# A matmul step of the RWKV branch and a chain step moved within one layer's written order

## The chip, the cores and the metric

The kernel runs on one core of a Trainium2 chip, out of eight. The metric is the device time of one execution in microseconds (us). The engines are TensorE (PE: matmul; PEld: its weight loads, which overlap), VectorE (DVE), ScalarE (ACT), GpSimd (POOL) and SyncE (SP), which issues the DMAs. They run at the same time, each through its own list of instructions in the order written, and wait for each other by semaphores. Matmul results go to PSUM, eight banks of 128 x 512 fp32.

## The reference

Two decoder layers over 512 positions of width 1024. Each layer takes an RMS norm, projects to 4160 columns, feeds four groups of heads, gates each with SiLU, and projects back with a residual:

```
h = rmsnorm(x, norm_w);  proj = h @ w_in
y_rwkv = rwkv7_time_mix(...) * silu(gate)     # 4 heads of 64
y_conv = short_conv_mix(...) * silu(gate)
y_moba = moba_attention(...) * silu(gate)     # causal, T5 bias
y_ret  = retention_chunkwise(...) * silu(gate)
x = x + concat(y_rwkv, y_conv, y_moba, y_ret) @ w_out
```

A final RMS norm follows. The RWKV group is a recurrence over time with a 64 x 64 state per head:

```
s_kk = state @ kk_t
state = state * w_t - s_kk (kk_t * a_t)^T + v_t k_t^T
y_t = state @ r_t
```

## The kernel before, in words

The activations are kept transposed in SBUF, as a rounded high part and a rest (act_hi, act_lo), and so are the weights (w_hi, w_lo). A projection of 128 columns is therefore 3 x 8 matmuls of 128 x 512 into one PSUM bank, in lines 773, 775 and 776. SyncE streams the weights; ScalarE (line 1286) and GpSimd (line 707) split them. The projections alternate between banks 0 and 1. Banks 2 to 7 serve the small work of the four groups.

The order of the work is written out by hand in layer_steps(). It returns one list of steps per layer, and each engine walks through the same list, doing its own part of every step that it has a function for. The second half of the list is made of slots: each of the last sixteen projections is cut into four quarters of six matmuls (step quarter), two quarters to a slot; mid[i] holds the steps between the two quarters of slot i, and after[i] those behind the second. Steps put in these places run on TensorE between products.

The RWKV recurrence is computed in 8 chunks of 64 positions. The steps that matter here:

- chunk_q (line 1077) computes two tiles q0 and q1, in banks 6 and 5. VectorE adds them to the queries in the step queries (line 1887); its four additions are line 1894. c = 0 reads q0, c = 1 reads q1, and each signals the bank as read behind its second addition.
- chunk_y1 (line 1080, by_chunk, lines 1104 and 1105) adds the two state-free terms of the output into y0 (bank 5) and y1 (bank 6), 64 small fp32 matmuls. It needs no result of the chain. Before the first matmul it calls begin for both banks.
- chain(c), c = 1 to 6, (line 1109 for TensorE, 1897 for VectorE) carries the state from chunk to chunk: four 64 x 64 matmuls into bank 7 (line 1121), then two multiply-adds on VectorE (line 1901), and the next chain step waits for them.
- chunk_y (line 1124) adds the state's part to y0 and y1. It waits for chain(6).

The attention runs in six units u: attend_scores(u) (TensorE line 1009, VectorE lines 1817 and 1822, ScalarE's exponential, line 1455), attend_norm(u) (VectorE, lines 1829 and 1832), attend_turn(u) (TensorE transposes, line 1020, evicted by ScalarE in line 1461), attend_values(u) (line 1036) and, after the last unit of a pair of heads, attend_out (VectorE, line 1840). Units 0 and 3 hold query blocks 0 and 1, units 1 and 4 block 2, units 2 and 5 block 3.

Which job uses a bank, and how often the bank must have been filled and read before, is counted by bank_jobs() in the order of the steps. The count makes a wait: begin(job) lets TensorE wait until every earlier job of the bank has been read:

```
def begin(job, layer):
    b, nf, nr, _ = locate(job, layer)
    if nr > 0:
        pe.wait_ge(bank_read[b], nr)
    return bank[b]
```

In slots 16 to 18 the list before the change reads: quarter(cc0, 0), attend_norm(2), queries, quarter(cc0, 1), quarter(cc0, 2), chain(5), attend_turn(2), quarter(cc0, 3), conv_c(0), attend_values(2), attend_out(0), attend_scores(3), chunk_y1, chain(6), quarter(cc1, 0), attend_norm(3), quarter(cc1, 1), quarter(cc1, 2), attend_turn(3), quarter(cc1, 3). Here cc0 and cc1 are two projections of the convolution group.

Of the kernel before, what the change touches and what calls it, by code (L numbers as in the profile page):

```python
# [108 lines left out]
UNITS = 2 * len(PARTS)  # L109
# [32 lines left out]
def layer_steps():  # L142

    s = [("k_pair",)]
    s += [("shift", "k0"), ("shift", "k1"), ("kk_input",), ("shift", "wa"), ("shift", "r0"), ("kk_square",),
          ("kk_norm",), ("kk_unit", 0), ("lora_tanh",), ("shift", "r1"), ("kk_unit", 1), ("lora",), ("shift", "v0"), ("decay_scan",), ("shift", "v1"),
          ("decay_exp",), ("factors", 0), ("gate", "rwkv", 0), ("factors", 1), ("gate", "rwkv", 1), ("factors", 2)]

    s += [("copy", "rq0"), ("copy", "rq1"), ("bonus",), ("rotate", "rq0"),
          ("copy", "rk0"), ("rotate", "rq1"), ("scores", 0), ("scores", 1), ("copy", "rk1"), ("rotate", "rk0"), ("to_rows", "v"), ("scores", 2),  # L150
          ("scores", 3), ("wide", 0, 0), ("wide", 0, 1), ("rotate", "rk1"), ("wide", 0, 2), ("wide", 0, 3),
          ("to_rows", "kap"), ("to_rows", "bet"), ("block_rows", 0), ("wide", 1, 0), ("wide", 1, 1), ("wide_out", 0), ("wide_out", 1),
          ("to_rows", "alp"), ("block_rows", 1), ("wide", 1, 2), ("wide", 1, 3), ("wide_out", 2), ("wide_out", 3), ("to_rows", "rk"),
          ("block_rows", 2)]

    last = [("gate", "ret", 0), ("gate", "ret", 1)] + [("copy", j) for j in ("mq0", "mk0", "mq1", "mk1")] + [("gate", "moba", 0), ("gate", "moba", 1)]
    last += [("conv_c", 0), ("conv_c", 1), ("conv_h", 0), ("conv_h", 1), ("conv_b", 0), ("conv_b", 1), ("gate", "conv", 0), ("gate", "conv", 1)]
    slots = 2 * len(last)  # L160
    mid, after = [[] for _ in range(slots)], [[] for _ in range(slots)]
    after[0] += [("retain_state",), ("retain_scores", 0), ("retain_scores", 1)]
    after[1] += [("centre_v",), ("inverse_eye",)]
    after[2] += [("retain_values",), ("retain_out", 0), ("retain_out", 1)]
    after[5] += [("ret_low",)]
    for i, step in [(INV0, ("inverse_x",)), (INV0, ("chunk_b",)),
                    (INV0 + 1, ("inverse_y",)), (INV0 + 1, ("inverse_yt",)),
                    (INV0 + 3, ("corner_x",)), (INV0 + 4, ("corner_t",)), (9, ("ret_stat",)), (10, ("chunk_uw",)),
                    (11, ("chunk_gh",)), (21, ("ln_square",)), (22, ("ln_var",))]:
        mid[i].append(step)  # L170
    for c in range(1, NCH - 1):


        if c % 2:
            mid[12 + c].insert(0, ("chain", c))
    after[9] += [("ret_root",), ("ret_recip", 0)]
    for u in range(UNITS + 1):


        if u > 0:  # L180
            mid[11 + 2 * u].append(("attend_turn", u - 1))
            after[11 + 2 * u].append(("attend_values", u - 1))
            if u % 3 == 0:
                after[11 + 2 * u].append(("attend_out", u // 3 - 1))
        if u in (1, 2):
            after[11 + 2 * u].append(("chain", 2 * u))
        if u < UNITS:
            (after[11 + 2 * u] if u else mid[10]).append(("attend_scores", u))
        if u == 3:
            after[11 + 2 * u] += [("chunk_y1",), ("chain", 2 * u)]  # L190
        if u < UNITS:
            (mid[12 + 2 * u] if u else after[11]).append(("attend_norm", u))
    mid[15].insert(1, ("chunk_q",))
    mid[16].append(("queries",))
    after[19].append(("chunk_y",))
    for i, step in [(10, ("ret_recip", 1)), (11, ("ret_recip", 2)), (12, ("ret_recip", 3)), (13, ("ret_finish", 0)), (14, ("ret_finish", 1)),
                    (21, ("conv_taps", 0)), (24, ("conv_taps", 1)), (22, ("ln_recip", 0)), (23, ("ln_recip", 1)), (25, ("ln_recip", 2)), (26, ("ln_recip", 3)),
                    (26, ("ln_scale", 0)), (27, ("ln_scale", 1)), (28, ("rwkv_finish", 0))]:
        after[i].append(step)
    for i in range(slots):  # L200
        step, job = last[i // 2], project_name(last[i // 2])
        s += [("quarter", job, 2 * (i % 2))] + mid[i] + [("quarter", job, 2 * (i % 2) + 1)]
        if i < slots - 1:
            s += [step] * (i % 2) + after[i]

    s += [("split_y", k) for k in Y_ORDER[:4]] + [("rwkv_finish", 1), ("split_y", 0), last[-1], ("conv_out", 0), ("split_y", 1), ("conv_out", 1)]
    s += [("split_y", k) for k in Y_ORDER[6:]] + [("out", q) for q in range(5)] + [("out_end",)]
    return s
# [5 lines left out]
def project_name(step):  # L214

    kind = step[0]
    if kind == "gate":
        return f"{step[1]}_g{step[2]}"
    if kind in ("conv_c", "conv_h", "conv_b"):
        return {"conv_c": "cc", "conv_h": "ch", "conv_b": "cb"}[kind] + str(step[1])  # L220
    return step[1]


Y_ORDER = [6, 7, 4, 5, 0, 1, 2, 3]
ROW_ORDER = [3, 2, 0, 1]
STEPS = layer_steps()


# [1871 lines left out]
```

## Time and profile before

| | us |
|---|---|
| median of 3 runs | 582.18 |
| lowest and highest | 581.69, 582.97 |
| the profiled execution, whole | 581.69 |
| its span, first to last instruction | 579.9 |
| TensorE busy | 571.4 |
| VectorE busy | 370.6 |
| ScalarE busy | 275.1 |
| GpSimd busy | 249.7 |

The profile is of one execution. Times in it count from the first instruction, so 1.8 us of the execution's time lie outside its span. The first layer takes the first half, the second the rest; the place of the change is near 195 us in the first layer and near 476 us in the second. Ends of matmuls are modelled and overlap the next start.

### The profile page before, as it was taken

To read this page: it belongs to the slowest core of one execution; us is meant where nothing else is said; L and a number is where in the kernel's file an instruction comes from. 1 tells how busy PE (TensorE), PEld (TensorE's weight loads), DVE (VectorE), ACT (ScalarE), POOL (GpSimd) and SP (SyncE) were. 2 spreads that over 40 slices of the span, in tenths; PEclk is the share of its full clock that TensorE was granted. 3 is DMA by queue.
4 is the path that set the end of the run, shared out by engine and by line. 5 is a ranking of instruction groups with operands and counts; after the bars stand their busy time and mean duration, and the time that the engine had idled before them with its cause. 6 is when DMAs were issued, how large, how long until landed. Compare 5 with 4: busy or idle time off the path is not lost. (4 is left out here: it accounts for less than half of the span.)

```text
span 579.9 us, 12191 instructions
## 1 busy us (share of the span) xinstructions
PE 571.4 (99%) x4988; PEld 467.2 (81%) x4988; DVE 370.6 (64%) x624; ACT 275.1 (47%) x551; POOL 249.7 (43%) x197
## 2 busy tenths in 40 slices
PE   9999999999999999999999999999999999999995
PEld 7978888888777777888898788888878778788884
DVE  4999975582276747774544897946434874778163
ACT  6485331345273565534657643324536334745253
POOL 5846451045923313436335555402395313145340
PEclk9999999999999999999999999999999999999999
DMA  9556725056422122353534433422744121224513
GB/s 283 160 153 184 227 74 119 0 129 148 110 76 73 43 68 58 113 170 135 163 121 133 110 85 98 108 48 85 153 112 111 37 74 40 72 73 146 181 41 141
DMA packets 103372, 64.61 MB, mean 111 GB/s; under 512 B 29152, under 2 KB 94228, under 8 KB 103189
## 3 DMA queue, kind: packets, MB, share of 16 engines
q1 hardware_dynamic: 103316, 63.83, 39.5%
q8 instruction: 40, 0.66, 0.5%
q14 instruction: 16, 0.12, 0.1%
HBM read 55.68 MB, written 8.14 MB: 110 GB/s over the span
## 5 line engine op out<-in xcount | busy, mean ns | idle before, releaser
L707 POOL TENSOR_TENSOR w_lo<-w_raw,w_hi 128x512 fp32r<-128x512 f32 x156 | 217.2, 1412 | 291.4 <-ACT w_hi L1286 290.0
L773 PE MATMUL bank<-act_hi,w_hi 128*128 128x512 f32 x432 | 173.1, 401 | 0.0
L776 PE MATMUL bank<-act_lo,w_hi 128*128 128x512 f32 x432 | 168.5, 390 | 0.3 <-issue 0.3
L775 PE MATMUL bank<-act_hi,w_lo 128*128 128x512 f32 x416 | 162.3, 390 | 0.0
L1286 ACT ACTIVATE w_hi<-w_raw 128x512 fp32r<-128x512 f32 x140 | 80.2, 621 | 73.7 <-PE bank L858 28.2
L773 PEld LDWEIGHTS bank<-act_hi,w_hi 128*128 128x128 f32 x432 | 81.1, 188 | 24.3 <-issue 7.8
L776 PEld LDWEIGHTS bank<-act_lo,w_hi 128*128 128x128 f32 x432 | 81.1, 188 | 18.0 <-issue 0.7
L775 PEld LDWEIGHTS bank<-act_hi,w_lo 128*128 128x128 f32 x416 | 78.2, 188 | 14.8
L1212 PE MATMUL bank<-w_hi,act_hi 128*128 128x512 f32 x128 | 50.0, 391 | 0.0
L1214 PE MATMUL bank<-w_hi,act_lo 128*128 128x512 f32 x128 | 49.8, 389 | 0.0
L1213 PE MATMUL bank<-w_lo,act_hi 128*128 128x512 f32 x128 | 49.8, 389 | 0.0
L1985 DVE TENSOR_TENSOR x_or_y<-x_or_y,bank 128x512 f32<-128x512 f32 x16 | 11.0, 688 | 37.5 <-PE bank L1214 37.5
L1394 ACT ACTIVATE pages<-bank 128x512 f32<-128x512 f32 x16 | 9.5, 596 | 42.1 <-PE bank L776 42.1
L1214 PEld LDWEIGHTS bank<-w_hi,act_lo 128*128 128x128 f32 x128 | 24.0, 188 | 5.0
L1212 PEld LDWEIGHTS bank<-w_hi,act_hi 128*128 128x128 f32 x128 | 24.0, 188 | 5.0
L1213 PEld LDWEIGHTS bank<-w_lo,act_hi 128*128 128x128 f32 x128 | 24.0, 188 | 4.9
L1455 ACT ACTIVATE pages<-pages,small 128x128 f32<-128x128 f32 (+3 forms) x32 | 17.9, 559 | 18.6 <-DVE small L1822 18.6
L1752 DVE SCALAR_TENSOR_TENSOR x_or_y<-x_or_y,bank 128x512 f32<-128x512 f32 x16 | 10.9, 683 | 23.6 <-ACT x_or_y L1360 23.4
L856 PE MATMUL bank<-w_hi,act_hi 128*128 128x512 f32 x64 | 25.5, 398 | 0.0
L858 PE MATMUL bank<-w_hi,act_lo 128*128 128x512 f32 x64 | 25.0, 390 | 0.0
L857 PE MATMUL bank<-w_lo,act_hi 128*128 128x512 f32 x64 | 24.9, 390 | 0.0
L1817 DVE SCALAR_TENSOR_TENSOR pages<-bank,bias 128x128 f32<-128x128 f32 (+3 forms) x32 | 14.7, 481 | 16.0 <-PE bank L1009 15.7
(217 smaller groups left out, 949.7 us busy)
## 6 DMA issues: line engine op xcount, KB each, us to landing
w_raw<-in_w_in_dram SPq DMA_DIRECT2D x62, 512.0 KB, 4.0
w_raw<-in_w_out_dram SPq DMA_DIRECT2D x16, 512.0 KB, 3.8
pages<-in_x_dram SPq DMA_DIRECT2D x4, 512.0 KB, 6.0
x_or_y<-in_x_dram SPq DMA_DIRECT2D x4, 512.0 KB, 4.0
x_scratch<-x_or_y SPq DMA_DIRECT2D x4, 512.0 KB, 2.9
x_or_y<-x_scratch SPq DMA_DIRECT2D x4, 512.0 KB, 3.7
out_dram<-pages SPq DMA_DIRECT2D x8, 256.0 KB, 2.2
bias_scratch<-pages SPq DMA_DIRECT2D x1, 1280.0 KB, 7.9
```

The costliest lines, as they stand in the source:

```text
L707: ins = pool.tensor_tensor(low, raw, w_hi[:, i % HI, k, 0:n].bitcast(F32), ALU.subtract)
L773: mm(b[:, :], hi, act_hi[:, k, :], start=n == 0, stop=False)
L775: mm(b[:, :], lo, act_hi[:, k, :], start=False, stop=False)
L776: ins = mm(b[:, :], hi, act_lo[:, k, :], start=False, stop=n == KT - 1)
L856: mm(o, act_hi[:, n, tc], w_hi[:, :, n, :], start=n == 0, stop=False)
L857: mm(o, act_hi[:, n, tc], w_lo[:, :, n, :], start=False, stop=False)
L858: ins = mm(o, act_lo[:, n, tc], w_hi[:, :, n, :], start=False, stop=n == KT - 1)
L1212: mm(b[:, :], act_hi[:, k, tc], hi[:, wc], start=first, stop=False)
L1213: mm(b[:, :], act_hi[:, k, tc], lo[:, wc], start=False, stop=False)
L1214: ins = mm(b[:, :], act_lo[:, k, tc], hi[:, wc], start=False, stop=last)
L1286: go(w_hi[:, i % HI, k, 0:n], w_raw[:, i % RAW, k, 0:n], ACT.Copy).then_inc(s("w_high"), 1)
L1455: go(pb, pb, ACT.Exp, bias=row_max[:, n:n + 1], accum_out=row_sum[:, n:n + 1]).then_inc(s("prob"), 1)
```

## The change

chunk_y1 moves from behind attend_scores(3) in after[17] to mid[17], between chain(5) and attend_turn(2). chain(6) stays in after[17], but now stands ahead of attend_scores(3) in place of behind it and chunk_y1. The list of slot 17 then reads: quarter(cc0, 2), chain(5), chunk_y1, attend_turn(2), quarter(cc0, 3), conv_c(0), attend_values(2), attend_out(0), chain(6), attend_scores(3), quarter(cc1, 0). attend_norm keeps its place. The counts of the banks follow the list: y0 and y1 are still the jobs behind q1 and q0 in banks 5 and 6.

```diff
@@ -166,7 +166,7 @@
-                    (11, ("chunk_gh",)), (21, ("ln_square",)), (22, ("ln_var",))]:
+                    (11, ("chunk_gh",)), (17, ("chunk_y1",)), (21, ("ln_square",)), (22, ("ln_var",))]:
         mid[i].append(step)
@@ -182,13 +182,10 @@
-        if u in (1, 2):
+        if u in (1, 2, 3):
             after[11 + 2 * u].append(("chain", 2 * u))
         if u < UNITS:
             (after[11 + 2 * u] if u else mid[10]).append(("attend_scores", u))
-        if u == 3:
-            after[11 + 2 * u] += [("chunk_y1",), ("chain", 2 * u)]
-        if u < UNITS:
             (mid[12 + 2 * u] if u else after[11]).append(("attend_norm", u))
```

## Rows read from the trace of the kernel before

**Rows 1.** The page: busy us, share and count; granted TensorE clock in 40 slices.

```profile
PE 571.4 (99%) x4988; PEld 467.2 (81%) x4988; DVE 370.6 (64%) x624; ACT 275.1 (47%) x551; POOL 249.7 (43%) x197
...
PEclk9999999999999999999999999999999999999999
```

**Rows 2.** Waits of TensorE, whole span: who <- for whom: us, times, longest.

```profile
PE bank L741 <- POOL pages L681: 1.0, 1, 1.0
PE bank L1102 <- issue: 0.7, 1, 0.7
PE bank L776 <- issue: 0.3, 1, 0.3
```

**Rows 3.** Timeline of TensorE, first layer: start us, us, engine, line, tiles, count.

```profile
194.44 0.45 PE L1121 MATMUL bank<-pages 64*64 64x64 f32 x8
194.82 1.09 PE L1020 MATMUL bank<-constants,pages 128*128 128x128 f32 x8
...
197.24 1.10 PE L1036 MATMUL bank<-pages 128*64 128x128 f32 x16
198.26 0.88 PE L1009 MATMUL bank<-pages 64*64 64x128 f32 x16
198.96 0.33 PE L1104 MATMUL bank<-pages 64*64 64x64 f32 x6
...
200.82 0.22 PE L1121 MATMUL bank<-pages 64*64 64x64 f32 x1
...
200.94 0.34 PE L1121 MATMUL bank<-pages 64*64 64x64 f32 x5
201.21 0.50 PE L773 MATMUL bank<-act_hi,w_hi 128*128 128x512 f32 x1
...
205.44 0.82 PE L1020 MATMUL bank<-constants,pages 128*128 128x128 f32 x6
```

**Rows 4.** Timeline of VectorE there; one stretch: us, busy (x), clock, DMA, GB/s.

```profile
194.49 1.41 DVE L1894 TENSOR_TENSOR pages<-pages,bank 128x256 f32<-128x256 f32 x4
195.82 0.47 DVE L1901 SCALAR_TENSOR_TENSOR pages<-bank,chunk_decay,pages 128x64 f32<-128x64 f32 x2
...
198.38 0.69 DVE L1840 SCALAR_TENSOR_TENSOR x_or_y<-bank,x_or_y 128x512 f32<-128x512 f32 x1 [2.08 <-PE bank L1036]
199.19 0.62 DVE L1817 SCALAR_TENSOR_TENSOR pages<-bank,bias 128x128 f32<-128x128 f32 x2
...
201.55 0.47 DVE L1901 SCALAR_TENSOR_TENSOR pages<-bank,chunk_decay,pages 128x64 f32<-128x64 f32 x2
...
202.79 0.55 DVE L1832 TENSOR_SCALAR pages<-pages,small 128x128 f32<-128x128 f32 x2
...
190.28:195.90 5.62, 5.19 (x13) 1.00 0.37 96
```

**Rows 5.** Timeline, second layer: two places where TensorE waits for another engine.

```profile
496.67 0.87 ACT L1461 ACTIVATE pages<-bank 128x384 f32<-128x384 f32 x2
...
497.68 0.88 PE L1036 MATMUL bank<-pages 128*64 128x128 f32 x12
...
504.04 0.49 DVE L1832 TENSOR_SCALAR pages<-pages,small 128x512 f32<-128x512 f32 x1
...
504.58 0.42 PEld L1020 LDWEIGHTS bank<-constants,pages 128*128 128x128 f32 x4 [0.20 <-DVE pages L1832]
504.64 1.19 PE L1020 MATMUL bank<-constants,pages 128*128 128x128 f32 x8
```

**Rows 6.** Timelines of TensorE and of VectorE in the second layer.

```profile
475.47 0.45 PE L1121 MATMUL bank<-pages 64*64 64x64 f32 x8
...
475.52 1.41 DVE L1894 TENSOR_TENSOR pages<-pages,bank 128x256 f32<-128x256 f32 x4
```

**Rows 7.** TensorE by stretches at the end: us, busy (x), granted clock, DMA, GB/s.

```profile
575.00:576.00 1.00, 0.00 (x0) 1.00 0.99 379
...
578.00:579.90 1.90, 0.00 (x0) 0.50 0.53 201
```

## The prediction

> **What bounds the kernel now.** I read the page's busy shares first. TensorE is busy 99% of the span at a granted clock of 9 tenths or more in every slice, the next engine 64% [rows 1]. The list of waits by engine comes second. It names almost nothing for TensorE: 1.0 us at the start, and later one gap of 0.7 us and one of 0.3 us put down to its own issue [rows 2]. So nothing on another engine can shorten the kernel unless TensorE waits for it, and any new wait of TensorE is paid in full. The timeline of TensorE and of VectorE around the moved steps comes third, because records of TensorE overlap (128 of them, of 0.22 us each, start within 1.86 us in chunk_y1 [rows 3]): a short wait doesn't show as idle time, and I go by the starts.
>
> The change touches one place per layer. TensorE's order there is now [rows 3]: chain(5) from 194.44, attend_turn(2) from 194.82, six products, attend_values(2) from 197.24, attend_scores(3) from 198.26, chunk_y1 from 198.96, chain(6) from 200.82, products from 201.21, attend_turn(3) from 205.44. Afterwards it is chain(5), chunk_y1, attend_turn(2), products, attend_values(2), chain(6), attend_scores(3), products, attend_turn(3).
>
> **Part 1: the work moved.** No instruction is added or removed on any engine, and no DMA, no ScalarE, GpSimd or SyncE step moves. chunk_y1 is 64 fp32 calls, 128 records per layer; from its first start to chain(6)'s it takes 200.82 - 198.96 = 1.86 us [rows 3]. It takes this from its old place and pays it at the new one: 0 in the sum. The kinds of tile on TensorE change as often as before: chain(5) and chunk_y1 are both 64*64 tiles ahead of the 128*128 transposes, and chain(6) and attend_scores(3) are 64*64 ahead of products. The last chain record starts 0.15 us before what follows it in both places (194.44 + 0.45 - 0.22 = 194.67 against 194.82; 200.94 + 0.34 - 0.22 = 201.06 against 201.21). An exit behind the 128-column scores, with records of 0.28 us in place of 0.22, may cost 0.06 more; a joint of two 64*64 steps less may give as much back. I take 0, with bounds of -0.1 and +0.1 per layer.
>
> **Part 2: the wait that chunk_y1 takes with it.** chunk_y1 writes y0 into bank 5 and y1 into bank 6, and asks for both banks before its first matmul. The jobs before it in these banks are q1 (bank 5) and q0 (bank 6), and VectorE reads them in the step queries, the four additions of line 1894. At the old place they were long read: 195.90 against 198.96. At the new place TensorE arrives as soon as chain(5) is issued. chain(5)'s last record starts at 194.67, so chunk_y1 could start at 194.68. VectorE starts the four additions at 194.49 and ends them at 194.49 + 1.41 = 195.90 [rows 4]. The one that counts first in the code is the last one: bank 5 holds q1, the second pair read.
>
> VectorE can't be earlier. From 190.28 to 195.90 it works almost without a hole through attend_scores(2), attend_norm(2) and then queries, 5.19 us busy of 5.62 [rows 4], and everything upstream of chain(5) is untouched by the change, so these times stand.
>
> The price of the release: at 504.04 + 0.49 = 504.53 VectorE ends a normalisation that TensorE waits for; the weight load starts at 504.58 and the matmul at 504.64, so 0.05 us plus 0.06 [rows 5]. That gives a first chunk_y1 matmul at 195.90 + 0.11 = 196.01, and a stall of 196.01 - 194.68 = 1.33 us. The bounds: 1.2 us, if the weight load is the only cost and the tail of chain(5) is hidden behind it, and 1.5 us, if the restart of an empty array is as slow as the slowest restart in these rows (ScalarE ends at 496.67 + 0.87 = 497.54, TensorE starts at 497.68, 0.14) and a first record is longer besides. In the second layer chain(5) starts at 475.47, 0.05 us before the four additions at 475.52, exactly as in the first (194.44 and 194.49) [rows 6], so the stall is the same: 2 x 1.33 = 2.66 us.
>
> **What is queued behind the wait.** TensorE runs in its written order, so attend_turn(2) stands behind chunk_y1 and starts at about 196.01 + 1.86 + 0.15 = 198.02 in place of 194.82. ScalarE's eviction of the transposes, attend_values(2), the eviction of cc0 and its weight preparation all follow TensorE and move by the same 3.2 us, of which 1.86 comes back where chunk_y1 no longer stands. GpSimd and the weight loads only get more time.
>
> **Part 3: chain(6) ahead of attend_scores(3).** On TensorE it waits for chain(5)'s read on VectorE, which starts at 195.82 and ends by 196.3; it comes at about 201.5 then, so no wait. On VectorE the 0.4 us of chain(6) (201.55 to 201.94) move ahead of the scores. The gap from attend_scores(3) to attend_turn(3) on TensorE shrinks, and here a second wait could appear. I count from the start of attend_values(2), as 0. TensorE: scores start at 1.02 and chunk_y1, chain(6) and scores cost 3.97 before the products (201.21 - 197.24). Without chunk_y1's 1.86 that is 2.1, and attend_turn(3) comes 205.44 - 201.21 = 4.23 later, at 6.33; its second half, which needs the second head, some 0.3 later. VectorE: attend_out ends at 199.07 - 197.24 = 1.83 [rows 4], chain(6) at about 2.15, the scores then start at 2.16 in place of 199.19 - 197.24 = 1.95. The last normalisation ended at 202.79 + 0.55 = 203.34, so 6.10, of which some 0.2 us was for chain(6) standing in between; with 0.21 added and 0.2 taken off it ends at about 6.1. It is needed at about 6.6. Cover left: 0.5 us in place of 2.1. Cost 0; if the cover fails, no more than some 0.3 us per layer.
>
> **Downstream.** After attend_turn(3) all engines stand to each other as before. Nothing there stops for anything but its predecessors, which move with TensorE; the waits of rows 5 (496.67 to 497.68, and at 504.5) come from ScalarE and VectorE chains that start at TensorE's own scores. So the delay isn't given back.
>
> **The sum.** 0 + 2.66 + 0 = +2.7 us on the profiled execution: span 579.9 to 582.6, its time 581.69 to 584.35. The median of the runs is 0.49 above the profiled one, so 582.18 + 2.66 = 584.8 us.
>
> **The clock.** TensorE's granted clock is 1.00 around the place, and at the end of the kernel it is still 1.00 from 575 to 576, a whole microsecond in which TensorE has no matmul; in the last 1.9 us it is 0.50, that is 1.2 in place of 2.4 GHz [rows 7]. A pause of that length leaves the clock where it is, and the stall of 1.3 us is little longer, so by these rows it costs nothing beyond itself. The Trainium skill (TensorE: Matmul & The Clock Gate, "A second HAM failure mode: psum-queue depth-cycling") says that short repeated idle spells between matmul groups can make the clock swing between its two levels. This kernel would have only one more such spell per layer. By that rule the sum would be the one of the third rival; the traces so far don't bear it out.
>
> **Rivals.**
> 1. The wait isn't there, or VectorE is through in time: TensorE meets bank 5 free. It decides at 194.68, the moment that TensorE gets there; the trace has the read at 195.90, and VectorE has no work that could go. For it speaks only that I infer TensorE's arrival from records with modelled ends. Then only part 1 is left: -0.2 to +0.2, so 582.2 us, not slower. Chance 0.13, of which 0.04 faster by over 0.2% and 0.09 within it (0.2% is what a measurement of this kernel can tell from no change, here 1.2 us).
> 2. Part of the stall is repaid: TensorE's small waits behind it vanish because others gain time: the release of 0.14 us at 497.68, and at 504.64, where the transposes take 1.19 us in place of the 1.09 at 194.82 [rows 3, 5]. It would give 584.8 - 2 x 0.24 = 584.3 us. Against it: they start from TensorE itself. Chance 0.06.
> 3. More than the stall: attend_turn(3) comes before its normalised rows (+0.3 per layer, 585.4 us), or the clock falls to its lower level in the pause. The slow stretch at the end holds at least 1.9 us; the same after each stall would cost half of it, 0.95 per layer, and twice that much if it lasts twice as long: 584.8 + 1.9 = 586.7, up to 588.6 us. Chance 0.07 together.
>
> **Numbers.** The forecast holds 0.74 by itself, 583.9 to 585.7 (stall 1.2 to 1.5 us per layer, part 1 at +-0.1 per layer, and the runs' own spread of about 0.5). With rival 2 and the near half of rival 3 in it, the range of 583.4 to 586.0 holds a little over 0.8. Faster 0.04, same 0.09, slower 0.87.
>
> **What the profile of the changed kernel would show.** A wait of TensorE at line 1104 on VectorE's line 1894, about 1.1 us of idle time in each layer (less than the stall by the pipelined tail), and none before. VectorE's four additions at 194.5 as now. attend_turn(2) at about 198.0 in the first layer, cc1's first product at 202.5, 1.3 after 201.21, and everything from there 1.3 later; from the second place on 2.7 later. attend_turn(3) without a wait. I am wrong if line 1104 starts before 195.9, if line 1894 starts earlier, if a wait of TensorE behind the place is new or gone, or if the granted clock falls below 1.00 near 196.

## The result and the profile after

| | before | changed |
|---|---|---|
| median of the runs, us | 582.29 (4 runs) | 585.75 (4 runs) |
| lowest and highest | 581.69, 582.97 | 584.31, 586.02 |
| profiled execution, whole; span | 581.69; 579.9 | 585.21; 583.4 |

The ratio is 1.0054, with a 95% interval of 1.0037 to 1.0072: the change made the kernel 2.2 to 4.2 us slower. A second measurement of the same two kernels, on another occasion, gave 1.0049 (1.0037 to 1.0062). The forecast was 584.8 us, slower, in a range of 583.4 to 586.0.

In the changed kernel every line behind the edited lines has a number lower by 3: chunk_y1 is in lines 1101 and 1102, queries in 1891, the transposes in 1017, the products in 770, 772 and 773. The waits of TensorE over the whole span (who waited, for whom: us in total, times, longest), of the changed kernel; before's are [rows 2]:

```profile
PE bank L1101 <- DVE pages L1891: 2.1, 2, 1.1
PE bank L738 <- POOL pages L678: 1.0, 1, 1.0
PE bank L1099 <- issue: 0.7, 1, 0.7
PE bank L773 <- issue: 0.5, 1, 0.5
PE bank L1033 <- ACT pages L1458: 0.3, 2, 0.2
```

The first line is new and is the forecast one: chunk_y1 waits twice, once in each layer, for VectorE's additions that read q0 and q1. The timeline of TensorE at the first place, changed kernel, to be laid beside [rows 3]:

```profile
194.90 0.45 PE L1118 MATMUL bank<-pages 64*64 64x64 f32 x8
196.41 0.37 PE L1101 MATMUL bank<-pages 64*64 64x64 f32 x8 [1.06 <-DVE pages L1891]
...
198.57 1.17 PE L1017 MATMUL bank<-constants,pages 128*128 128x128 f32 x8
199.50 0.47 PE L770 MATMUL bank<-act_hi,w_hi 128*128 128x512 f32 x1
...
201.06 1.09 PE L1033 MATMUL bank<-pages 128*64 128x128 f32 x16
202.08 0.38 PE L1118 MATMUL bank<-pages 64*64 64x64 f32 x5
202.25 0.32 PE L1006 MATMUL bank<-pages 64*64 64x128 f32 x1
...
203.11 0.50 PE L770 MATMUL bank<-act_hi,w_hi 128*128 128x512 f32 x1
...
207.35 0.82 PE L1017 MATMUL bank<-constants,pages 128*128 128x128 f32 x6
```

and VectorE there, to be laid beside [rows 4]:

```profile
194.95 1.41 DVE L1891 TENSOR_TENSOR pages<-pages,bank 128x256 f32<-128x256 f32 x4
...
202.20 0.69 DVE L1837 SCALAR_TENSOR_TENSOR x_or_y<-bank,x_or_y 128x512 f32<-128x512 f32 x1 [5.45 <-PE bank L1033]
202.81 0.47 DVE L1898 SCALAR_TENSOR_TENSOR pages<-bank,chunk_decay,pages 128x64 f32<-128x64 f32 x2
203.25 0.62 DVE L1814 SCALAR_TENSOR_TENSOR pages<-bank,bias 128x128 f32<-128x128 f32 x2
...
206.62 0.55 DVE L1829 TENSOR_SCALAR pages<-pages,small 128x128 f32<-128x128 f32 x2
```

The four additions start 0.05 us behind chain(5), as before, and end at 196.36; chunk_y1 starts at 196.41. From chain(5) to cc1's first product it is 203.11 - 194.90 = 8.21 us in place of 201.21 - 194.44 = 6.77, so the place costs 1.44. The second place, by the same rows:

```profile
477.63 0.45 PE L1118 MATMUL bank<-pages 64*64 64x64 f32 x8
...
479.14 0.37 PE L1101 MATMUL bank<-pages 64*64 64x64 f32 x8 [1.06 <-DVE pages L1891]
...
481.31 1.09 PE L1017 MATMUL bank<-constants,pages 128*128 128x128 f32 x8
```

**A table that needs one idea.** TensorE issues the same matmuls in the same order outside the two places. So I subtract, record by record, the start in one trace from the start of the same record in the trace of before. The difference is flat wherever nothing differs and steps up where something is lost. The steps at the two places, and the difference outside of them, are:

| trace | ahead of place 1 | place 1 | between | place 2 | at the last matmul |
|---|---|---|---|---|---|
| before, second trace | +0.10 | 0.00 | +0.17 | 0.00 | +0.28 |
| changed | +0.45 | 1.46 | +0.25 | 1.35 | +3.52 |
| changed, second trace | -0.30 | 1.47 | +0.47 | 1.38 | +3.07 |
| chunk_y1 alone | +0.37 | 1.45 | +0.20 | 1.38 | +3.41 |
| chain(6) alone | +0.09 | 0.10 | +0.20 | 0.09 | +0.49 |
| queries first | -0.11 | 0.17 | +0.46 | 0.08 | +0.59 |
| chunk_y1 behind the transposes | +0.86 | 1.71 | +0.18 | 0.56 | +3.31 |
| the same, second trace | +0.56 | 1.43 | +0.04 | 0.54 | +2.58 |
| chunk_y1 earlier | +0.57 | 5.98 | +0.33 | 3.37 | +10.26 |
| the same, second trace | +0.69 | 4.63 | +0.30 | 4.78 | +10.38 |
| chunk_y1 late | +1.22 | 0.25 | +0.17 | 0.25 | +1.90 |

Place 1 is measured from 189.6 to 208.1 us of before's time, place 2 from 455.5 to 488.0; a row adds up to its last column within 0.05, which arises behind place 2. The two places of the change come to 2.81 and 2.85 us and repeat to 0.03. What lies ahead of place 1 doesn't repeat, not even between two traces of one kernel.

### The profile page after: what moved, and what is told of

The parts are those of the page before. It is cut to its first block and busy times, and to the rows that moved or that the text cites. A ratio compares the mean times of both kernels' runs of the same rounds, so it can differ in the third digit from the quotient of the medians.

```text
span 583.4 us, 12191 instructions
## 1 busy us (share of the span) xinstructions
PE 572.7 (98%) x4988; PEld 468.0 (80%) x4988; DVE 368.5 (63%) x624; ACT 275.4 (47%) x551; POOL 250.2 (43%) x197
## 5 line engine op out<-in xcount | busy, mean ns | idle before, releaser
L1357 ACT ACTIVATE x_or_y<-bank 128x512 f32<-128x512 f32 x16 | 9.6, 598 | 31.0 <-PE bank L773 31.0
```

## Experiments

Each ratio is to the kernel before, from runs on the same chip, with its 95% interval. "At the places" means the columns of the table above.

**1. chunk_y1 alone.** chain(6) goes back behind attend_scores(3).

```diff
-        if u in (1, 2, 3):
+        if u in (1, 2):
             after[11 + 2 * u].append(("chain", 2 * u))
         if u < UNITS:
             (after[11 + 2 * u] if u else mid[10]).append(("attend_scores", u))
+        if u == 3:
+            after[11 + 2 * u].append(("chain", 2 * u))
+        if u < UNITS:
```

> One half of the change: chunk_y1 moves to its new place, chain(6) stays behind attend_scores(3). Theory (the wait of chunk_y1 for the read of bank 5 is the whole price): a wait at chunk_y1's first matmul of about 1.1 us of idle time in each layer, its first start 1.51 us behind chain(5)'s, cc1's first product 1.35 to 1.45 us late per place, and the time 2.8 us above before (585.1), within 0.3 of the changed kernel. Rival A (the order of chain(6) and attend_scores(3) holds the part that the forecast of 2.66 lacks against the measured 3.46): the wait is the same but the time is only 2.0 to 2.3 above before.

Measured: 585.52 us, ratio 1.0057 (1.0044 to 1.0070); 1.45 and 1.38 us at the places, the same wait of 1.06. That is the whole change again. Rival A falls.

**2. chain(6) alone.** chunk_y1 stands behind attend_scores(3), chain(6) ahead of it.

```diff
-                    (11, ("chunk_gh",)), (17, ("chunk_y1",)), (21, ("ln_square",)), (22, ("ln_var",))]:
+                    (11, ("chunk_gh",)), (21, ("ln_square",)), (22, ("ln_var",))]:
...
+        if u == 3:
+            after[11 + 2 * u].append(("chunk_y1",))
+        if u < UNITS:
```

> The other half: chain(6) ahead of attend_scores(3), chunk_y1 behind it, where nothing waits for banks 5 and 6. Theory: no wait of TensorE at chunk_y1, products of cc1 at the same distance from attend_values(2) as before (3.97 us, within 0.1), time within 0.3 us of before (582.3). Rival A: 0.5 to 0.8 us above before. Rival B (the price belongs to the new neighbours of chunk_y1, not to the wait): no change either, so this run is for A.

Measured: 582.75 us, ratio 1.0006 (0.9997 to 1.0014), 0.10 and 0.09 us at the places, no wait at chunk_y1. The timed runs can't tell this from nothing (0.4 us by the medians, a little over the expected 0.3); the traces can, and it is 0.1 us per place.

**3. queries first.** The changed kernel, with VectorE's read of the banks moved up.

```diff
-    mid[16].append(("queries",))
+    mid[16].insert(0, ("queries",))
```

> The changed kernel, with the step queries ahead of attend_norm(2), so that VectorE reads q0 and q1 while it would otherwise come to the normalisation: its four additions should start near 193.5 and end near 194.9, just about when chain(5) is issued, and the normalisation ends 1.4 us later, near 196.0, before the transposes need it at 196.9. Theory (the wait is the price): the wait at chunk_y1 falls from 1.06 us to 0.3 or less per layer, and the time to within 0.6 us of before (582.3 to 582.9). Rival B (TensorE pays for chunk_y1 between chain(5) and the transposes, by tile changes or the array's state, whoever reads the bank): the time stays at 585, as in the changed kernel. A mixed case: if the delayed normalisation stops the transposes instead, the wait moves to line 1017 and up to 0.7 us per layer stay.

Measured: 582.99 us, ratio 1.0010 (1.0001 to 1.0019), so by the ratios 2.6 us below the changed kernel, with all of its order on TensorE kept. By the medians it is 0.7 us above before, where at most 0.6 was expected. The wait list of this kernel has no line for chunk_y1. VectorE and TensorE at the first place:

```profile
192.81 1.41 DVE L1891 TENSOR_TENSOR pages<-pages,bank 128x256 f32<-128x256 f32 x4
...
194.92 0.49 DVE L1829 TENSOR_SCALAR pages<-pages,small 128x512 f32<-128x512 f32 x1
```

```profile
194.33 0.45 PE L1118 MATMUL bank<-pages 64*64 64x64 f32 x8
...
194.62 0.33 PE L1101 MATMUL bank<-pages 64*64 64x64 f32 x6
...
196.74 1.15 PE L1017 MATMUL bank<-constants,pages 128*128 128x128 f32 x8
```

The read ends at 194.22, 0.7 us earlier than expected; chunk_y1 starts at 194.62, directly behind chain(5)'s last record, and the normalisation is through at 195.41, before the transposes at 196.74. The additions take over a spell of 0.29 us in which VectorE had waited for ScalarE's exponential; for the rest they push the normalisation back, by 0.9 us against chain(5), and nobody waits for it. This is the experiment that decides: the place and the neighbours are the changed kernel's, only the reader of the bank comes earlier, and the loss is gone but for 0.17 and 0.08 us. Rival B falls. In the changed kernel chain(5)'s last record starts at 194.90 + 0.45 - 0.22 = 195.13, so chunk_y1 could start at 195.14 and starts at 196.41: the wait by starts is 1.27 us; with these 0.17 and 0.08 it makes 1.44 and 1.35, the whole price of the two places.

**4. chunk_y1 behind the transposes.** A smaller dose of the same wait.

```diff
-                    (11, ("chunk_gh",)), (17, ("chunk_y1",)), (21, ("ln_square",)), (22, ("ln_var",))]:
+                    (11, ("chunk_gh",)), (21, ("ln_square",)), (22, ("ln_var",))]:
...
+    mid[17].append(("chunk_y1",))
```

> The changed kernel with chunk_y1 behind attend_turn(2) in place of ahead of it: TensorE arrives 0.85 us later, so less of the same wait is left. Theory: the stall is 196.0 less 195.65, 0.35 us per layer, and a further change of tile kind costs 0.1 to 0.15 and the restart 0.15: together 0.5 to 0.6 per layer, time 1.0 to 1.3 above before (583.4). Rival B: a price per place that doesn't go with the arrival, 2.8 or more above before, since there is one change of tile kind more here.

Measured: 584.74 us, ratio 1.0040 (1.0028 to 1.0052). This expectation was missed, by 1.2 us. Place 2 gave 0.56, as expected, place 1 gave 1.71, and the trace says where the rest went:

```profile
PE bank L1100 <- issue: 1.4, 1, 1.4
...
PE bank L1103 <- issue: 1.0, 1, 1.0
PE bank L774 <- issue: 0.5, 1, 0.5
```

Line 1103 is the second matmul of chunk_y1 here. It doesn't wait for an engine: TensorE's own issue stops for 0.96 us just before the step ends.

```profile
196.81 0.37 PE L1102 MATMUL bank<-pages 64*64 64x64 f32 x8
...
199.95 0.27 PE L1103 MATMUL bank<-pages 64*64 64x64 f32 x2 [0.96 <-issue]
200.16 0.50 PE L771 MATMUL bank<-act_hi,w_hi 128*128 128x512 f32 x1
```

**5. The same kernel again**, for the gap.

> The kernel with chunk_y1 behind attend_turn(2) once more, for a second trace. The first had 1.71 us of delay at the first place, of which 0.96 in a gap of issue inside chunk_y1, and 0.56 at the second, as forecast. Theory D (the supply of instructions, which depends on the program's place and so repeats): the gap of about 1 us at the first place again. Rival: it was an accident of that execution, and both places show 0.5 to 0.6.

Measured: one run, 584.27 us; 1.43 and 0.54 us at the places, a gap of 0.68 us at the same instruction. That it comes, and where, belongs to the program; its length changes from execution to execution.

**6. chunk_y1 earlier.** A larger dose. The edit removes the entry of slot 17 as above and adds:

```diff
+    after[16].append(("chunk_y1",))
```

> The changed kernel with chunk_y1 one half slot earlier, between quarter(cc0, 1) and quarter(cc0, 2): TensorE arrives at about 192.85 and VectorE still reads bank 5 until 195.90. Theory: a stall of 196.0 less 192.85, 3.15 us per layer, and 0.35 for two more changes between tile kinds and 0.15 for the restart: 3.6 per layer, 7.2 us above before (589.5). Rival B (the price belongs to the neighbours chain(5) and attend_turn(2)): below the changed kernel's time. On the clock: the granted clock stays at 1.00 in the pause; if it falls, the matmuls behind the pause take twice as long and the time is several us above 589.5.

Measured: 591.47 us, ratio 1.0148 (1.0133 to 1.0164). That is 2.0 us more than expected. The wait went from 1.06 to 2.80 us in both layers. Place 2 cost 3.37 us, near the expected 3.6. Place 1 cost 5.98, because the clock fell towards the end of the pause. TensorE by stretches (us, busy and count, granted clock, DMA share, GB/s):

```profile
193.00:196.00 3.00, 0.72 (x4) 0.96 0.70 171
196.00:197.00 1.00, 0.48 (x16) 0.50 0.04 11
...
198.00:200.00 2.00, 2.00 (x85) 0.50 0.00 0
...
202.00:204.00 2.00, 2.00 (x17) 0.86 0.03 8
```

```profile
483.80:487.00 3.20, 3.15 (x132) 1.00 0.02 5
```

**7. The same kernel again**, for the clock.

> The kernel with chunk_y1 one half slot earlier once more. In its first trace the granted clock fell to 0.50 for 6.8 us behind the first pause of 3.2 us and stayed at 1.00 behind the second, equally long. If the fall is a matter of when the pause lies within what the chip looks at, it comes in this trace at one of the two pauses, at both or at none; where it comes, the place costs 5.5 to 6.2 us, elsewhere 3.3 to 3.5. If it always follows the first pause, that place has a reason of its own.

Measured: one run, 592.09 us. This time the clock fell at both, for a shorter time: at 196.2 us, within the pause, and at 482.9, 0.3 us behind its end (second trace):

```profile
196.50:203.00 6.50, 6.37 (x151) 0.76 0.02 5
...
483.80:487.00 3.20, 3.20 (x92) 0.61 0.00 0
```

Of four pauses of one length, three were followed by a fall. They cost 5.98, 4.63 and 4.78 us, the fourth 3.37; the last two lie below the 5.5 to 6.2 that was expected where the clock falls. So a wait of this size has no one price, and the first place has no reason of its own.

**8. chunk_y1 late.** The entry of slot 17 is removed and the step stands just ahead of attend_values(2):

```diff
+    after[17].insert(0, ("chunk_y1",))
```

> The changed kernel with chunk_y1 behind quarter(cc0, 3), just ahead of attend_values(2): TensorE arrives at about 197.2, after the read of bank 5 at 195.9. Theory: no wait at chunk_y1, at most 0.15 us per layer for one more change between tile kinds; time 582.3 to 582.7, within 0.4 of before. Rival B in its wider form (chunk_y1 costs more at any place but its old one): 1 us or more above before.

Measured: 583.09 us, ratio 1.0011 (1.0002 to 1.0020), 0.25 us at each place, no wait, no gap. TensorE finds the bank already read. The 0.25 us is the price of one more group of small tiles by itself, between full-size matmuls, more than the 0.15 that I had set, and the time is 0.6 us above before in place of at most 0.4.

**9 and 10. Both kernels again.**

> The changed kernel once more, unchanged. It gives a second ratio and a second trace. Theory: 2.8 to 3.2 us above before, the stall at chunk_y1 the same to 0.1 us, and the parts of the first trace that lie outside the two places (0.48 us by 17 us into the span, 0.21 near 455 us) not the same in this one, since they come from the start and from single executions. Rival C (they belong to the change): 0.48 and 0.21 again at the same steps.

> The kernel before once more, unchanged, for a second trace. Theory: its starts of matmuls differ from the first trace of before by up to some 0.5 us that arises in the first 20 us, and by nothing at the two places. Rival C: no difference anywhere, so that the 0.7 us outside the places would be the change's.

Measured: 585.62 us, ratio 1.0049 (1.0037 to 1.0062), for the changed kernel, one run of 581.98 for the one before. The places repeat, the rest doesn't: by 174 us the second trace of the changed kernel is 0.3 us ahead of before's where the first was 0.45 behind. Rival C falls for the start. Near 455 us the step is 0.47 here, 0.25 in the first trace of the changed kernel, and 0.17 in the second trace of before, where nothing was changed, so it isn't the change's either. The gap at line 1099 and 773 (1102 and 776 before) is in every trace so far, before and after, with 0.7 to 1.5 and 0.3 to 0.7 us.

**11. chunk_gh cut in two**, on the kernel before.

```diff
-            layer += [("g0", 5, 1), ("g1", 6, 1), ("h0", 7, 1), ("h1", 4, 1)]
+            layer += [("g0", 5, 1), ("g1", 6, 1)]
+        elif kind == "chunk_h":
+            layer += [("h0", 7, 1), ("h1", 4, 1)]
...
+    after[11].insert(0, ("chunk_h",))
...
                     by_chunk("g")
+                def chunk_h():
                     by_chunk("h")
```

(VectorE's part of the step is divided in the same way, the reads of h0 and h1 going with chunk_h, and both engines get the new step.)

> The kernel before (not the changed one) with chunk_gh cut in two: the matmuls of g stay in their place, those of h come one quarter of products later. It tests the gaps that the trace puts down to TensorE's own issue, 0.7 to 1.4 us inside h near 169 us in every trace, and 0.3 to 0.7 just behind h near 451 us. Theory D (192 calls of small tiles in one go outrun the supply of instructions, so that products in between let it catch up): both gaps gone, 0.25 us per layer for the further change of tile kind, as measured with chunk_y1 ahead of attend_values(2); time 0.5 to 1.0 us below before. Rival E (the gaps come at fixed places of the program, whatever stands there): the gaps stay the same in size and the time is 0.3 to 0.6 above before.

Measured: 581.14 us against 582.28, ratio 0.9986 (0.9977 to 0.9995), faster than both kernels. By the ratio it is 0.8 us below before, as theory D has it, by the medians 1.1, a little more. The step that was cut has 96 calls, g's 32 and h's 64, which leave 192 records; the expectation took the records for calls. From the start of g to chain(1) this trace has 174.83 - 165.66 = 9.17 us in the first layer and 455.72 - 446.55 = 9.17 in the second; before had 175.88 - 166.10 = 9.78 and 456.91 - 447.61 = 9.30. In its list of waits the gaps of 0.7 and 0.3 are gone:

```profile
PE bank L744 <- POOL pages L684: 1.0, 1, 1.0
PE bank L822 <- DVE act_lo L1625: 0.2, 1, 0.2
PE bank L1110 <- issue: 0.2, 1, 0.2
```

A smaller one turned up in chunk_y1 of the second layer (line 1110 here), where the difference to before steps up by 0.49 us. So the gap is not tied to h: it moves with the instructions.

## Why the prediction was right

**The stall** (part 2) is the change's price, as forecast: the same two partners, in both layers, 1.06 us of idle time against "about 1.1". Experiment 3 shows it by taking the reason of the wait away, 4, 6 and 8 by moving TensorE's arrival by 1.0 us to later, 1.6 us to earlier and 2.6 us to later, which cost 0.56, 3.37 and 0.25 us at a place whose clock and issue were undisturbed. I had said a stall of 1.33 us and nothing else per layer. The stall by starts is 1.27; the places cost 1.46 and 1.35 (1.47 and 1.38 in the second trace), so the rest is 0.1 to 0.2.

By its terms, at place 1: the release was faster than I took it, chain(5) to chunk_y1 is 1.51 us in place of 1.57 (196.41 comes 0.05 behind the end of the additions; the 0.06 from weight load to matmul aren't seen). chunk_y1 itself was undersized: from its first start to the transposes it is 2.16 us (2.17 at place 2), and I had 1.86 + 0.15. The 1.86 was misread: it runs to chain(6)'s first record, and the last records of chunk_y1 start behind that one.

```profile
200.82 0.22 PE L1121 MATMUL bank<-pages 64*64 64x64 f32 x1
200.87 0.22 PE L1105 MATMUL bank<-pages 64*64 64x64 f32 x2
200.88 0.22 PE L1121 MATMUL bank<-pages 64*64 64x64 f32 x2
200.93 0.22 PE L1105 MATMUL bank<-pages 64*64 64x64 f32 x1
```

From first to last start it is 200.93 - 198.96 = 1.97, and 1.97 + 0.15 = 2.12 is what experiment 3 has (196.74 - 194.62), where the step follows chain(5) without a wait. Experiment 8 has 2.16 too, without any wait, so the further 0.04 us is no sign of a restart. From the transposes to attend_values(2) it is 2.49 (2.39 at place 2) in place of 2.42, from there to the product 2.05 in place of 2.10. In sum 8.21 against my 8.10.

Part 1, the work moved, was put at 0 with bounds of +-0.1 per layer. Measured without the stall it is 0.17 at place 1 and 0.08 at place 2, so the bound was broken at place 1. The difference between the places is in the transposes, 1.17 us (198.57) against 1.09 (481.31) in the rows of the result: one of the eight starts 0.19 us behind the one before it in place of 0.11. The last section says what that is.

**Part 3** held. attend_turn(3) has no wait; from attend_values(2) it starts at 207.35 - 201.06 = 6.29 us, forecast 6.33, and VectorE is through at 206.62 + 0.55 - 201.06 = 6.11, forecast about 6.1. Experiment 2 puts the price of this half, with chunk_y1 still behind the scores, at 0.1 us per place. In the changed order nothing of it is left: experiment 1, which doesn't have it, costs as much as the whole change.

**Not given back.** The difference to before stays flat behind place 1 to within 0.04 us up to the gap of issue near 451 us (1.91 us at 208, 1.95 at 450). Rival 2 is out. Its small wait for ScalarE is unchanged: line 1033's two waits in the list above are of 0.15 us each, and the matmul at 497.68 in before's trace has 0.15 us of idle time ahead of it too, just too short for before's list.

**The clock** (rival 3) was rightly priced at nothing for this change: it is 1.00 in both stretches with the 1.06 us wait.

```profile
194.50:199.00 4.50, 3.44 (x143) 1.00 0.30 89
477.20:481.50 4.30, 3.24 (x141) 1.00 0.33 96
```

But my reason was too generous. I took the end of the kernel, where the clock held through a pause, as cover; experiments 6 and 7 show it fall at pauses of 3.2 us from last start to next start, and the changed kernel's own end, where the last matmul starts at 576.89, shows it fall sooner than before's did (4.3 us behind the last start there, 2.4 here):

```profile
575.00:579.00 4.00, 2.28 (x11) 1.00 0.19 72
579.00:583.40 4.40, 0.00 (x0) 0.53 0.46 175
```

One trace of one pause was too little for a rule. The Trainium skill (TensorE: Matmul & The Clock Gate, "Why this matters for your kernels") asks for short gaps between bursts of matmuls, since a long one brings the clock back down. These traces agree, three times in four.

**The size.** The traces give 2.8 us at the places. The timed runs give 3.1 and 2.9 us by the ratios of the two comparisons (3.3 for experiment 1), 3.5 and 3.1 by the medians. The intervals of the ratios begin at 2.2 us and hold the 2.8, so no loss beyond the two places is shown. Part of the scatter may be the gap of issue near 169 and 451 us, whose length varies from execution to execution.

The idle time in the wait list (1.06) is 0.21 us less than the wait by starts (1.27), and 0.38 less than the place's cost (1.44), of which 0.17 isn't wait. The Trainium skill (Perfetto Trace Analysis, "Tensor Engine Instruction (MATMUL, LD_WEIGHTS)") says that the end of a matmul in a profile is an estimate and not an observation. The rows fit: chain(5)'s last record starts at 195.13 and is drawn to 195.35, which hides 0.2 us of the wait. Starts are the safer measure.

## What to carry to other kernels

Before moving a step that writes into a shared buffer, look up who empties the buffer and when that reader is done in its own engine's order; where the moved engine is the bound, release minus arrival is most of the price, 1.27 of 1.44 and 1.35 us here, as long as the clock holds. If the new order is wanted all the same, move the reader, as experiment 3 does: the wait cost 2.5 us in the two layers, and one line took it away. Compare two traces of one kernel record by record before any step of a few tenths is put down to a change.

## What the hardware showed

TensorE's issue can stop with no engine to wait for: 0.7 to 1.5 us near the end of 96 small matmul calls (192 records) in one go, 0.3 to 0.7 us behind the same step in the second layer, 0.96 and 0.68 us in one order of chunk_y1, 0.16 us of idle time in chunk_y1 of experiment 11. Cutting the dense step in two removed the first two. The page of each kernel lists the instruction transfers; here before's:

```profile
q8 instruction: 40, 0.66, 0.5%
```

That is 16 KB each, and for the 10246 instructions of TensorE (matmuls, weight loads, semaphore instructions) it is 256 to a transfer. Two things in the traces tie the gaps to these transfers. Counted over all of TensorE's instructions, every one of the 27 gaps in the thirteen traces stands ahead of a matmul whose number leaves the same remainder, 193, on division by 256. And every one ends 1.2 to 1.5 us behind the end of a transfer on q8, whatever its length: in experiment 4 transfers end at 169.28, 198.54 and 453.25 us, and the gaps at 170.69, 199.95 and 454.48. The slow transposes of place 1 have the same remainder, and in the changed kernel's trace they stand 1.5 us behind a transfer. In the kernel before that instruction lies inside chunk_y1, its transfer had ended 3.5 us earlier, and there is no gap.

So the evidence is strong that dense small matmuls used up a block of instructions before the next had come. It is from reading traces: no run changed the supply alone. The Trainium skill (Runtime: NRT & Kernel Launch, "Instruction fetch mechanics") says that fetching is hidden, because dispatch is slower than the fill. If that is what these gaps are, the traces don't agree with it there.
